# The first mixer's projections as three fp32r products, with the lower halves of the weights made by GpSimd

## What is computed

```
u = rms_norm(h, w_norm_mix)                      # (272, 1024)
proj = u @ w_in                                  # conf_a, conf_g, z, xbc, dt_raw, gates
c = conf_a * sigmoid(conf_g);  c = depthwise_conv(c, 31 taps);  c = silu(layer_norm(c))
branch_conf = c @ w_conf_out
xbc = silu(depthwise_conv(xbc, 7 taps));  y = bidir_ssd(xs, dt, B, C)   # scans both ways, 32 heads
y = rms_norm(y * silu(z));  branch_ssm = y @ w_ssm_out
merged = gates[0] * branch_conf + gates[1] * branch_ssm
h = h + merged @ w_out
h = h + expert_choice_ffn(rms_norm(h))           # 16 experts, some 400 MB of weights
```

## Time and profile before

| | |
|---|---|
| median of 3 runs | 2524.82 us (2522.86 to 2526.81) |
| the profiled execution, its own time | 2524.76 us |
| its span | 2522.7 us |
| mean granted TensorE clock | 0.963 of full speed |
| busy: PE, PEld, DVE, ACT, POOL | 2373.0, 1577.1, 1142.7, 674.9, 22.5 us |
| DMA | 677.03 MB, mean 268 GB/s |

### The profile page before, as it was taken

The page is one execution under the profiler, slowest core; times in us unless marked ns, Lnnn a source line. Parts: engine busy times, 40 slices in busy tenths (PEclk is TensorE's granted clock), DMA queues, the critical chain, the costliest instruction groups (busy, mean ns, idle before and its releaser), DMA issues. The chain is left out here.

```text
span 2522.7 us, 34246 instructions
## 1 busy us (share of the span) xinstructions
PE 2373.0 (94%) x13937; PEld 1577.1 (63%) x13937; DVE 1142.7 (45%) x2374; ACT 674.9 (27%) x1213; POOL 22.5 (1%) x38
## 2 busy tenths in 40 slices
PE   8999999989999888888898879999999999999998
PEld 6786777874222222222222236889999999888887
DVE  5657973131111111111111116238887776788887
ACT  2125564020000000000000002324454444454444
POOL 1000000000000000000000000000000000000000
PEclk9999999989999999999989989899999999999999
DMA  5365556737999999999999991324775555777775
GB/s 172 107 217 172 177 171 203 242 140 300 405 428 428 428 428 427 428 427 428 428 428 428 428 369 35 133 84 140 222 228 175 179 174 178 249 241 243 242 242 162
DMA packets 205420, 677.03 MB, mean 268 GB/s; under 512 B 15072, under 2 KB 137200, under 8 KB 180336
## 3 DMA queue, kind: packets, MB, share of 16 engines
q1 hardware_dynamic: 205296, 675.30, 72.3%
HBM read 657.40 MB, written 17.83 MB: 268 GB/s over the span
## 5 line engine op out<-in xcount | busy, mean ns | idle before, releaser
L549 PE MATMUL ps<-u,ring 128*128 128x272 f32 x1248 | 298.7, 395 | 4.1 <-DVE ring L387 2.9
L984 PE MATMUL ps<-ring,tokens 128*34 128x512 f32 x1248 | 273.6, 593 | 16.6 <-DMA ring<-in_w_up 16.6
L549 PEld LDWEIGHTS ps<-u,ring 128*128 128x128 f32 x1248 | 233.1, 190 | 55.8 <-issue 8.7
L2019 PE MATMUL ps<-m_hi,row_hi 128*128 128x256 f32 x1024 | 256.4, 288 | 0.8 <-ACT peer_s L2085 0.8
L1162 DVE TENSOR_TENSOR first_room<-first_room,ps 98x512 f32<-98x512 f32 x32 | 21.8, 682 | 505.7 <-PE ps L984 505.7
L2019 PE MATMUL ps<-m_lo,row_hi 128*128 128x256 f32 x1024 | 250.7, 283 | 0.0
L984 PE MATMUL ps<-extra_early,tokens 128*34 128x512 f32 x752 | 197.4, 676 | 14.7 <-DMA extra_early<-in_w_gate 11.8
L984 PEld LDWEIGHTS ps<-ring,tokens 128*34 128x34 f32 x1248 | 72.2, 112 | 215.2 <-issue 185.5
L1001 PE MATMUL ps<-ring,first_room 128*34 128x512 f32 x768 | 179.6, 614 | 25.5 <-DVE first_room L1166 23.0
L2019 PEld LDWEIGHTS ps<-m_hi,row_hi 128*128 128x128 f32 x1024 | 195.7, 191 | 1.6 <-issue 1.0
L2019 PEld LDWEIGHTS ps<-m_lo,row_hi 128*128 128x128 f32 x1024 | 196.1, 191 | 0.0
(11 more groups left out here) (398 smaller groups left out, 3015.7 us busy)
## 6 DMA issues: line engine op xcount, KB each, us to landing
ring<-in_w_down SPq DMA_DIRECT2D x48, 2048.0 KB, 22.4
ring<-in_w_up SPq DMA_DIRECT2D x47, 2048.0 KB, 24.5
ring<-in_w_gate SPq DMA_DIRECT2D x31, 2048.0 KB, 24.7
extra_early<-in_w_gate SPq DMA_DIRECT2D x31, 2048.0 KB, 18.5
ring<-in_w_in SPq DMA_DIRECT2D x36, 1024.0 KB, 5.4
extra_early<-in_w_up SPq DMA_DIRECT2D x16, 2048.0 KB, 25.7
extra_early<-in_w_down SPq DMA_DIRECT2D x16, 2048.0 KB, 25.4
rows<-in_peer_u SPq DMA_DIRECT2D x64, 512.0 KB, 3.7
```

What stands on the lines that cost most here:

```text
L549: last = pe.matmul(bank[:, 0:T], wt[:, k, c:c + P], src[:, k, :], start=k == 0, stop=k == kt - 1)
L984: last = pe.matmul(s.ps[HALF * j:HALF * j + CAP, 2 * c + u % 2, :], s.tokens[:, 2 * (u // 2) + k, :], rows[k][:, 1024 * c + 512 * j:1024 * ...
L2019: pe.matmul(out, hi[:, P * k:P * k + P], m[:, k, :], start=k == 0 and m is s.m2_hi, stop=False)
```

## The change

Each fp32 operand of a projection is split into an upper part, rounded to fp32r, and a lower part, the rest, also as fp32r. A product of fp32 becomes three products of fp32r: upper weights by upper activations, upper weights by lower activations, lower weights by upper activations.

- The upper parts of the weights are made by ScalarE (`round_weights`, an activation of 128x1024 elements for each 8 weight blocks), in two buffers used in turn; it waits until PE has used the buffer (`hi_used`) and until the lower part two places earlier is made.
- The lower parts (`lower_part`, a subtraction of two SBUF operands, 128x1024) are made by GpSimd for the `x`, `a`, `g`, `z` and `gate` tiles beyond the first four parts, 69 in all, and by VectorE (`dve_lower`) for the first four and for `conf`, `ssm` and `out`, 32 parts.
- The activations are split by ScalarE and VectorE: `u_hi`, `u_lo`, `conf_hi`, `conf_lo`, `y_hi`, `y_lo`, `m_hi`. `u_hi` and `u_lo` lie where `h` and `u` lay, so `h` is loaded again (`h_again`) ahead of the `out` tiles.
- The ring of the mixer's weights has 3 slots instead of 4. Two of the four expert units that were loaded between `ssm` tiles are loaded behind them.

```diff
+    def lower_part(eng, n):
+        return eng.tensor_tensor(lower_view(n), weights_of(n), upper_part(n).bitcast(F32), ALU.subtract)
...
-            pool.wait_ge(cb_out, GROUPS)
-            pool.memset(s.decay[:, :, :], 0.0).then_inc(clean, 1)
+            for n in on_pool:
+                if parts[n][0] == pos["a", 4]:
+                    pool.wait_ge(cb_out, GROUPS)
+                    pool.memset(s.decay[:, :, :], 0.0).then_inc(clean, 1)
+                pool.wait_ge(w_hi, n + 1)
+                lower_part(pool, n).then_inc(w_lo, 1)
...
-            before = {tiles[pos["ssm", m]][2]: m - 1 for m in range(1, 5)}
+            before = {tiles[pos["ssm", m]][2]: m + 1 for m in range(1, 3)}
...
+                if i == tiles[pos["ssm", 3]][2]:
+                    sp.wait_ge(tiled, pos["gate", 2 * KT - 1] + 1)
+                    sp.dma_start(s.h[:, :, :], hT).then_inc(h_again, 16)
...
+            for k in range(KT):
+                dve.wait_ge(u_hi, k + 1)
+                dve.tensor_tensor(s.u_lo[:, k, :], s.u[:, k, :], s.u_hi[:, k, :].bitcast(F32), ALU.subtract)\
+                   .then_inc(u_lo, 1)
+            for n in on_dve[0:4]:
+                dve_lower(n)
...
                 dve.tensor_tensor(s.u[:, m, :], ps[:, t % 2, 0:T], s.gates[:, m, :], ALU.mult).then_inc(evac_d, 1)
+                dve_lower((parts_of[pos["conf", m + 2]] if m + 2 < KT else parts_of[pos["ssm", 0]])[m == KT - 1])
+                if m >= 3:
+                    for i in range(3 * m - 9, min(3 * m - 6, 13)):
+                        lower_y(i)
...
-                    for k in range(kt):
-                        last = pe.matmul(bank[:, 0:T], wt[:, k, c:c + P], src[:, k, :], start=k == 0, stop=k == kt - 1)
+                    for n in parts_of[t]:
+                        k0 = parts[n][2]
+                        pe.wait_ge(w_hi, n + 1)
+                        for src, sem in ((hi, hi_sem), (lo, lo_sem)):
+                            for k in range(KT):
+                                if m == 0:
+                                    pe.wait_ge(sem, k0 + k + 1)
+                                last = pe.matmul(bank[:, 0:T], upper_part(n)[:, k, :], src[:, k0 + k, :],
+                                                 start=src is hi and k0 + k == 0, stop=False)
+                        last.then_inc(hi_used, 1)
+                        pe.wait_ge(*lower[n])
+                        for k in range(KT):
+                            last = pe.matmul(bank[:, 0:T], lower_view(n)[:, k, :], hi[:, k0 + k, :],
+                                             start=False, stop=n == parts_of[t][-1] and k == KT - 1)
...
+            def round_weights(n):
+                act.wait_ge(*w.ready[parts[n][1]])
+                if n >= 2:
+                    act.wait_ge(hi_used, n - 1)
+                    act.wait_ge(*lower[n - 2])
+                act.activation(upper_part(n), weights_of(n), ACT.Copy).then_inc(w_hi, 1)
+
             def evacuate(t):
                 kind, m, _, _ = tiles[t]
+                for n in parts_of.get(t, ()):
+                    round_weights(n + 2)
                 act.wait_ge(tiled, t + 1)
...
                         act.activation(s.conf[:, k, :], s.conf[:, k, :], ACT.Silu, bias=s.col("ln_b")[:, k:k + 1]).then_inc(silus, 1)
+                        act.wait_ge(silus, k + 1)
+                        act.activation(s.conf_hi[:, k, :], s.conf[:, k, :], ACT.Copy).then_inc(c_hi, 1)
```

More of the change, by code:

```diff
@@ L96, in add @@
     def add(self, src, a, b):
-        slot = (len(self.units) + self.first) % RING
+        slot = (len(self.units) + self.first) % self.ring
         self.loads[slot] += 1
@@ L229, in mixer @@
     tiles, ada = plan_mixer(s)
+    w.first = (w.ring - len(w.units)) % w.ring
     pos = {(kind, m): t for t, (kind, m, _, _) in enumerate(tiles)}
@@ L312, in _ @@
             s.load_expert_unit(sp, 0, AHEAD - 1, 0)
-            sp.wait_ge(tiled, pos["out", 3] + 1)
+            for u in range(AHEAD, AHEAD + 2):
+                s.load_expert_unit(sp, 0, u)
+            sp.wait_ge(tiled, pos["out", 5] + 1)
             s.load_expert_unit(sp, 0, AHEAD + 4)
@@ L486, in _ @@
             store_ada(HALVES - 1)
+            for k in range(KT):
+                dve.wait_ge(c_hi, k + 1)
+                dve.tensor_tensor(s.conf_lo[:, k, :], s.conf[:, k, :], s.conf_hi[:, k, :].bitcast(F32), ALU.subtract)\
+                   .then_inc(c_lo, 1)
+            for m in range(2):
+                dve_lower(parts_of[pos["conf", m]][0])
             for m in range(KT):
@@ L499, in _ @@
                 t = pos["ssm", m]
+                later = parts_of[pos["ssm", m + 1]] if m + 1 < KT else parts_of[pos["out", 0]] + parts_of[pos["out", 1]]
+                dve_lower(later[0])
                 dve.wait_ge(tiled, t + 1)
@@ L637, in _ @@
             last.then_inc(sum0, 1)
[L639 to L645, removed]
+            pe.wait_ge(w_hi, 2)
+            for src, sem in ((s.u_hi, u_hi), (s.u_lo, u_lo)):
+                for k in range(KT):
+                    pe.wait_ge(sem, k + 1)
+                    for t in range(2):
+                        last = pe.matmul(ps[:, t, 0:T], upper_part(t)[:, k, :], src[:, k, :], start=src is s.u_hi and k == 0, stop=False)
+                        if src is not s.u_hi and k == KT - 1:
+                            last.then_inc(hi_used, 1)
+            for t in range(2):
+                pe.wait_ge(*lower[t])
+                for k in range(KT):
+                    last = pe.matmul(ps[:, t, 0:T], lower_view(t)[:, k, :], s.u_hi[:, k, :], start=False, stop=k == KT - 1)
+                last.then_inc(tiled, 1)
             for t in range(2, pos["a", 0]):
@@ L780, in _ @@
             act.activation(s.std[:, :], ps[:, 7, 0:T], ACT.Sqrt, bias=s.eps[:, 0:1], scale=1.0 / D).then_inc(std0, 1)
+            for n in range(2):
+                round_weights(n)
+            for k in range(KT):
+                act.wait_ge(normed, k + 1)
+                act.activation(s.u_hi[:, k, :], s.u[:, k, :], ACT.Copy).then_inc(u_hi, 1)
             act.wait_ge(small_in, 16)
@@ L844, in _ @@
             act.activation(s.std[:, :], ps[:, 7, 0:T], ACT.Sqrt, bias=s.eps[:, 0:1], scale=1.0 / INNER).then_inc(ystd, 1)
+            for m in range(5, KT):
+                round_weights(parts_of[pos["conf", m]][0])
+            for n in parts_of[pos["ssm", 0]]:
+                round_weights(n)
             for m in range(KT):
+                for n in parts_of[pos["ssm", m]]:
+                    round_weights(n + 2)
+                act.wait_ge(evac_d, KT + m + 1)
+                act.activation(s.m_hi[:, m, :], s.u[:, m, :], ACT.Copy).then_inc(m_hi, 1)
+            for m in range(KT):
+                if m + 2 < KT:
+                    round_weights(parts_of[pos["out", m + 2]][0])
                 act.wait_ge(evac_d, 2 * KT + m + 1)
@@ L2224, in build_program @@
         s.std, s.gain, s.mod = keep("std", [P, T]), keep("gain", [P, KT]), keep("mod", [P, 48])
+        with ExitStack() as inner:
+            s.u_hi, s.u_lo = (opener(inner)(k, [P, KT, T], F32R) for k in ("u_hi", "u_lo"))
         s.h, s.u = keep("h", [P, KT, T]), keep("u", [P, KT, T])
```

117 lines of the change are left out of this document (90 added, 27 removed).

## The result

| | before | after |
|---|---|---|
| median | 2525.82 us (2522.86 to 2526.97, 4 runs) | 2621.34 us (2610.89 to 2640.03, 4 runs) |
| profiled execution, its span | 2524.76, 2522.7 us | 2619.99, 2618.3 us |
| mean granted clock | 0.963 | 0.937 |
| experts' stream starts at | 581.54 us | 677.80 us |

The change makes the kernel slower: ratio 1.0388, interval 1.0328 to 1.0448. The direction and the exclusion of VectorE and GpSimd were forecast. The size was not: 2564 us was forecast with a range up to 2605, and 57 us more were measured. All of it is lost before the experts: their stream starts 96.3 us later, and the span is 95.6 us longer.

The account below looks back on a forecast made before the run. It took PE to be nearly full in the `x` tiles, PE and VectorE in the first 12 pairs, PE alone after. Stage terms 3 + 20.7 - 2.6 + 36.4 - 18.3 = +39.2 us on 2524.76 gave 2564 us, range 2490 to 2605.

Parts of the forecast that it names:

- The exclusion: GpSimd's subtractions and VectorE's instructions with two SBUF inputs exclude each other for whole instructions; with about 2.1 us a part, chance 0.60.
- The rivals in which it doesn't hold: Rival: VectorE and GpSimd don't exclude each other here, so GpSimd's parts hide; 2486 us, faster, chance 0.14.
- GpSimd is quick: Rival: GpSimd takes 1.06 us a part and still excludes VectorE; 2502 us, faster, chance 0.08.
- the near balance: Rival: more cover and a part of 1.5 us end within 0.2% of no change; chance 0.04.
- Two coincidences in the trace of before: Stretched VectorE instructions ended with GpSimd's: beside the `decay` fill (0.14 us apart) and at 1503.44 us (0.01 us apart).
- The price of a part: One GpSimd subtraction of 1024 elements was taken as 2.1 us, twice the one-input time of 1.06 us.
- The cover: First 12 pairs: half of VectorE's 28.5 us of PSUM reading and idle time hides GpSimd's 50.4 us, leaving +36.4 us.
- faster PE gives nothing here: First 12 pairs: a pair runs in VectorE's order, so PE's quicker products were counted as no gain.
- The start: First products wait for split activations (+0.6 us) and `dt` grows by 2.4 us, so the convolution starts +3 us later.
- now PE is already ahead: Stretch to the first scan: the convolution's next piece starts some 11.5 us after the last instead of 21.69 us.
- The ring of 3 slots costs nothing in this sum: PE frees weight slots well before VectorE lets it go on; with PE in the lead, about 1 us a unit.
- the third rival: VectorE's unbroken steps keep GpSimd out and PE waits for lower parts, six times; +20 us, 2584 us, chance 0.14.

Follow-up runs that it names:

- fill_thrice: The changed kernel with each of GpSimd's 69 subtractions replaced by three fills that read nothing, lower parts left out as zeros; 2527.39 us, ratio 1.0008.
- side_fills: The kernel before plus three unused GpSimd fills in each of 63 places, one place a tile; 2529.79 us, ratio 1.0018.
- once_fillers: The changed kernel with one fill for each GpSimd subtraction, plus 4 unused fp32 products on PE in each of the first 11 pairs; 2509.29 us, ratio 0.9933.
- fillers: The changed kernel plus 8 unused fp32 products on PE in each of the first 11 pairs; 2622.72 us, ratio 1.0382.
- fill_once: The changed kernel with each of GpSimd's 69 subtractions replaced by one fill of 1024 elements, lower parts left out; 2529.95 us, ratio 1.0010.
- side_reads: The kernel before plus 63 unused GpSimd subtractions of two SBUF operands, 1024 elements each, one a tile; 2608.05 us, ratio 1.0324.

## Why the prediction was right and wrong

The forecast's terms, what the changed kernel did, and the same with fills (`fill_thrice`, whose traced execution lies 12 us under its median), in us against before:

| stage | forecast | after | with fills |
|---|---|---|---|
| start of the convolution | +3 | +10.9 | +2.0 |
| `x` tiles | +20.7 | +22.0 | -7.1 |
| to the first scan | -2.6 | +18.6 | +0.2 |
| first 12 pairs | +36.4 | +55.4 | +9.5 |
| last four pairs, `conf`, `ssm`, `out` | -18.3 | -10.6 | -13.4 |
| sum | +39.2 | +96.3 | -8.8 |

Two terms make up 40 of the 57 us by which the sum was short: the stretch to the first scan (21 us) and the first 12 pairs (19 us).

- **The exclusion** was right, and it is shown: the difference of the last two columns down to the pairs is 8.9 + 29.1 + 18.4 + 45.9 = 102.3 us for 69 subtractions, with what follows from them (the lower clock too). By the medians it is 94 us, 1.4 us each. The rivals in which it doesn't hold (2486 us) or in which GpSimd is quick (2502 us, 1.06 us a part) are out, and so is the near balance. Two coincidences in the trace of before, 0.01 and 0.14 us apart, carried this. But one of them isn't what it was read as: that fill was at work beside a `tensor_scalar`. Fills hold those (a group of four took 2.68 us in `side_fills`, 1.42 without) and leave alone the steps with two SBUF inputs. So it is no evidence for the lock that mattered, and the chance rested on one short instruction.
- **The price of a part** was too low: 2.1 us taken, 2.34 us at the least and 2.52 in the middle of the 69 measured, within the bounds of 1.06 and 2.8. The Trainium skill's page GPSIMD Engine Reference, section "Performance versus the Vector engine", by whose figure the estimate was 2.25 us, was nearer than the rule of twice one input.
- **The cover** in the pairs was right. 24 parts of 2.4 to 2.5 us are 58 to 60 us; VectorE's busy time grew by 44.5 (176.03 - 131.58), so 13 to 16 us of them cost nothing, where 14 were forecast. With the right price the term is about +45. The other 11 us are VectorE's waits, 26.8 us where the kernel before had 15.8, nearly all of it for ScalarE's decays (24.3 against 13.3). With fills, which don't hold these steps, they were 24.5 us.
- **The clock** was missing from the sum altogether. The step of the pairs' term that failed is "faster PE gives nothing here" (beside the low price): it put the effect at nothing and assumed that PE at least stays as it was. With less to do PE waits more, its granted clock falls to 0.83 in the pairs (two levels, 1.2 and 2.4 GHz), and a scan takes up to 4.56 us instead of 2.55; a late scan makes the decays late, for which VectorE waits. `once_fillers` puts 16.0 us on this in the pairs where nothing is held. In the changed kernel the four pairs at clock 0.92 took 15.2 us each, where 15.3 were forecast, and the six at 0.77 took 17.7; `fillers`, made to isolate it, gained nothing. The clock isn't all of it: in `once_fillers`, at 0.99, the pairs were still 6.1 us longer than before, and with fills, at 0.97, 9.5. ScalarE has 22 us more of work ahead of the decays, which likely has a share; how the rest divides is open.
- **The start** (+3) left out that the five subtractions begin beside the `dt` chain. A forecast of +2 to +3 was right for the rest (`fill_thrice` +2.0); each of three short instructions then waited a whole subtraction, 2.44 us for 0.36. In turn these five parts are not in the `x` tiles, where 25 were counted and 20 ran: there a low price and a high count cancelled. VectorE was held for 39 us where 47.5 were forecast, and it waited for 10.9 us where 1 was. So +20.7 against +22.0 is luck.
- **To the first scan** (forecast -2.6, measured +18.6, the largest miss) two steps failed. The first is "now PE is already ahead", so that the next piece of the convolution starts 11.5 us after the last: it started after 24.2 us, and after 22.3 with fills. ScalarE rounds a tile's weights as soon as they land, and 11.4 of these 24.2 us are its waits for them (24.1 in the whole stretch, 31.4 with fills); in the kernel before ScalarE waits there for PE, and no wait for a load shows. "The ring of 3 slots costs nothing in this sum" took no such waits into account; whether the ring causes them is open. The second is the 19.6 us by which GpSimd was to lengthen VectorE's work here: VectorE was busy for 25.43 us, as before (25.38). Instead the third rival, VectorE's unbroken run that keeps GpSimd out, which had 0.14, happened, in another size: PE waited 13.4 us at one place, not 3 us more at six. In the pairs, where 8 steps follow each other, single parts took 2.3 to 4.1 us.
- **Behind the pairs** `conf` was within 0.4 us, `ssm` and `out` within 2; the four last pairs gave 0.5 instead of 4. A product of fp32r took 0.125 us, not 0.122 (eight in 1.00 us), which is 1.2 us of what `ssm` missed.

The Trainium skill's page SBUF — State Buffer, section "Who interferes with whom", says that a VectorE instruction with two SBUF inputs contends with a GpSimd instruction that reads SBUF and not with one that only writes it, and that one with at most one SBUF input is free, outside the modes in which it uses two ports. The runs agree with all three: 653 ns beside reads, 495 beside fills, and 429 and 492 for the PSUM readers. The prediction left that exception out and said that no row shows the rule on one input, but the `tensor_scalar` of the earlier trace rows has one tensor input in SBUF and was held by a fill. The page also says that issue order decides who blocks. That fits the short turns at 41.71 us; when a waiting instruction gets its turn in a run of steps without a gap, as at 205.33 us, it doesn't say.

## What to carry to other kernels

GpSimd is no free engine for two-input work while VectorE works on two SBUF operands: count its whole duration, less what falls on VectorE's idle time and PSUM readers, as VectorE's, and if VectorE can do the piece in half the time, let it. Price a gain of PE by the stage: it was worth 10.8 us where PE alone was full and nothing where VectorE was, and freeing PE there can cost, since its granted clock falls. Compare traces only with an eye on where each execution lies among its kernel's runs. A small test tells in advance: the added instruction, unused, on the kernel before (`side_reads`) cost 83 us, and needs nothing of the change; the whole change then cost 96. The two figures don't measure the same: the change also gives PE less to do and ScalarE more, and gains behind the pairs.

## What the runs showed of the hardware that was not expected

- The turns fall in two ways. Beside short chained instructions of VectorE (128x192) GpSimd and VectorE alternated one for one. Beside 44 steps of 0.41 us that follow without a gap one GpSimd subtraction lasted 16.84 us, to the end of the run, and VectorE lost nothing. Beside 24 such steps in the `x` tiles one lasted 9.58 us and ended before they did (111.52 us). What decides was not tried.
- 44 unused fp32 products, spread over 11 pairs, made a kernel 20.7 us faster (`once_fillers` against `fill_once`).
- In the pairs of the changed kernel the scan's 24 records took 4.56 us where PE had waited 4.7 us ahead of them, and 2.55 us where it had waited 0.6 us:

```profile
270.49 4.56 PE L724 MATMUL ps<-ring,xbc 128*64 128x272 f32 x24 [4.73 <-DVE ring L416]
...
373.72 2.55 PE L724 MATMUL ps<-ring,xbc 128*64 128x272 f32 x24 [0.59 <-DVE ring L416]
```
